# Sixteen modulation units as float32 weighted sums on VectorE, and a projection ring whose low part is written in place

## The reference, cut to what matters

```
mod   = silu(c)     @ w_ada + b_ada        # 1024 -> 6 * 1024
mod_c = silu(c_ctx) @ w_ada + b_ada
sh1, sc1, ga1, sh2, sc2, ga2 = split(mod, 6)
hl = rms_norm(x)   * (1 + sc1)  + sh1      # latents
hc = rms_norm(ctx) * (1 + csc1) + csh1     # context
```

## Time and profile before

| what | value |
|---|---|
| median of 3 runs | 1674.27 us (1671.4 to 1674.83) |
| span of the profiled execution | 1675.7 us |
| PE busy | 1390.9 us, 83% |
| DVE busy | 1021.4 us, 61% |
| ACT busy | 802.2 us, 48% |
| POOL busy | 133.2 us, 8% |
| mean granted TensorE clock | 0.916 |

### The profile page before, as it was taken

How to read it: one execution, slowest core, us unless ns; L and a number is a source line. 1 busy time by engine, 2 the same in 40 slices (tenths; PEclk the granted TensorE clock), 3 DMA queues, 4 the chain that set the end, 5 groups by cost and what they waited for, 6 DMA issues and landing times.

```text
span 1675.7 us, 23258 instructions
## 1 busy us (share of the span) xinstructions
PE 1390.9 (83%) x8782; PEld 1247.4 (74%) x8782; DVE 1021.4 (61%) x1204; ACT 802.2 (48%) x924; POOL 133.2 (8%) x126
## 2 busy tenths in 40 slices
PE   4797999796998989548588970699999999999980
PEld 2686899795898989437477950588889888898870
DVE  5638320598013332366732379688888888888865
ACT  5533220333122332536522231377887778887752
POOL 0000000210000000100000440100110001001103
PEclk9998989998998899879878995799999999999995
DMA  9110000002123323000040157599999999999965
GB/s 343 64 61 17 35 1 1 1 0 76 50 76 126 126 76 127 0 0 0 1 157 21 31 219 283 176 348 377 381 370 382 380 373 374 369 383 382 382 218 213
DMA packets 142118, 293.26 MB, mean 175 GB/s; under 512 B 4832, under 2 KB 94944, under 8 KB 139632
## 3 DMA queue, kind: packets, MB, share of 16 engines
q1 hardware_dynamic: 137456, 275.70, 45.5%
q0 software_dynamic: 4608, 16.78, 3.9%
HBM read 271.49 MB, written 20.97 MB: 175 GB/s over the span
## 4 chain that ended last, share of the span: by engine, by line
PE 68%; DVE 13%; ACT 5%; DMA 4%; issue 4%; SPq 3%; POOL 2%; DVEq 0%; POOLq 0%; ACTq 0%
PE psum L1870 18%; PE psum L1618 8%; PE psum L1659 5%; PE psum L1661 5%; PE psum L1660 5%; PE psum L1863 3%; PE psum L1861 3%; PE psum L1862 3%; SPq L517 2%; DMA e_raw<-w_e_up 2%; DVE w_lo L1054 2%; ACT w_hi L677 1%; DVE mask_add L1466 1%; DVE left L1469 1%; PE psum L1621 1%
## 5 line engine op out<-in xcount | busy, mean ns | idle before, releaser
L1486 DVE TENSOR_TENSOR e_lo<-e_raw,e_hi 128x2048 fp32r<-128x2048 f32 x192 | 434.1, 2288 | 50.9 <-ACT e_hi L987 49.8
L987 ACT ACTIVATE e_hi<-e_raw 128x2048 fp32r<-128x2048 f32 x192 | 363.5, 1914 | 76.6 <-PE psum L1870 46.3
L1659 PE MATMUL psum<-w_hi,h_hi 128*128 128x256 f32 x576 | 165.6, 287 | 0.5 <-issue 0.5
L1660 PE MATMUL psum<-w_hi,h_lo 128*128 128x256 f32 x576 | 164.5, 286 | 0.0
L1661 PE MATMUL psum<-w_lo,h_hi 128*128 128x256 f32 x576 | 164.4, 285 | 0.0
L1054 DVE TENSOR_TENSOR w_lo<-raw,w_hi 128x2048 fp32r<-128x2048 f32 x35 | 79.7, 2289 | 134.6 <-ACT w_hi L677 134.6
L1861 PE MATMUL psum<-e_hi,xt_hi 128*128 128x256 f32 x512 | 147.3, 288 | 0.0
L1863 PE MATMUL psum<-e_lo,xt_hi 128*128 128x256 f32 x512 | 144.8, 283 | 0.0
L1862 PE MATMUL psum<-e_hi,xt_lo 128*128 128x256 f32 x512 | 144.7, 283 | 0.0
L1659 PEld LDWEIGHTS psum<-w_hi,h_hi 128*128 128x128 f32 x576 | 112.3, 195 | 0.6 <-issue 0.6
L1660 PEld LDWEIGHTS psum<-w_hi,h_lo 128*128 128x128 f32 x576 | 112.1, 195 | 0.0
(11 more groups left out here) (343 smaller groups left out, 2965.2 us busy)
## 6 DMA issues: line engine op xcount, KB each, us to landing
e_raw<-w_e_gate SPq DMA_DIRECT2D x64, 1024.0 KB, 17.2
e_raw<-w_e_up SPq DMA_DIRECT2D x64, 1024.0 KB, 14.1
e_raw<-w_e_down SPq DMA_DIRECT2D x64, 1024.0 KB, 13.5
raw<-w_ada SPq DMA_DIRECT2D x16, 1024.0 KB, 5.5
raw<-w_in_units SPq DMA_DIRECT2D x15, 1024.0 KB, 4.8
ada_raw<-w_ada SPq DMA_DIRECT2D x8, 1024.0 KB, 12.2
xs<-x SPq DMA_DIRECT2D x4, 1024.0 KB, 13.8
raw<-w_out_units SPq DMA_DIRECT2D x4, 1024.0 KB, 5.0
```

The source lines that it names most:

```text
L987: act.activation(e_hi[u % EH][:], e_raw[u][:], ACT.Copy).then_inc(e_hi_ok, 1)
L1486: dve.tensor_tensor(e_lo[u][:], e_raw[u][:], e_hi[u % EH][:], ALU.subtract).then_inc(e_lo_ok, 1)
L1659: pe.matmul(o, x_hi[:, k, c], w_hi[n % 2][:, k, :], start=k == 0, stop=False)
L1660: pe.matmul(o, x_lo[:, k, c], w_hi[n % 2][:, k, :], start=False, stop=False)
```

## The change

Three edits go together.

1. The modulation units j = 8 to 23 leave the stream. They stand behind gq 2, gv0 3, gv1 3, o0 2, o1 2, r0 2 and r1 2. SP loads them to two raw buffers of their own (`ada_x`, at 16 and 24 KB of the ring). DVE multiplies each of the 8 blocks of 128 x 256 by its column of `c32` (silu of the latents' conditioning vector) and adds them up in float32 in `mod_acc` (four buffers): one `tensor_scalar` and seven `scalar_tensor_tensor`, each waiting for the one before. PE makes two products of 2 columns from the sum, with `one_c` (all ones), which adds over the partitions and lands as columns in `modps`. The context's column is no longer computed for these units. ACT has no part in it.
2. `w_lo[s]` has the address of `raw[s]`. The low part is written over the raw unit, and SP waits before loading unit n until PE has used unit n - 2 (`wait_used` moves from ACT to SP for n >= 10).
3. Addresses move: `h_ml`, `ml_ks`, `ml_c`, `sel_r` within the ring, and `pos_r2` to 16 KB of the ring. SP now loads `pos_r2` right behind `x_res`, and out2 and out3 behind `pos_r2`.

```diff
+ADA_COUNT = {"gq": 2, "gv0": 3, "gv1": 3, "o0": 2, "o1": 2, "r0": 2, "r1": 2}
...
+STREAM = [("ada", j) for j in ADA_FIRST] + [("in", j) for j in range(len(IN_UNITS))] + [("out", j) for j in range(4)]
...
-        w_hi = [at(f"w_hi{s}", AT_RING + (32 - 16 * s) * KB, [P, KC, UW], F32R) for s in range(2)]
-        w_lo = [at(f"w_lo{s}", AT_RING + (40 - 16 * s) * KB, [P, KC, UW], F32R) for s in range(2)]
+        w_lo = [at(f"w_lo{s}", AT_RING + 8 * KB * s, [P, KC, UW], F32R) for s in range(2)]
+        w_hi = [at(f"w_hi{s}", AT_RING + (32 + 8 * s) * KB, [P, KC, UW], F32R) for s in range(2)]
+        ada_x = [at(f"ada_x{s}", AT_RING + (16 + 8 * s) * KB, [P, KC, UW]) for s in range(2)]
+        mod_acc = at("mod_acc", AT_OUT + 58 * KB, [P, 4, UW])
...
             def load_unit(n):
                 if n >= 10:
-                    sp.wait_ge(hi_ready, n - 1)
-                    sp.wait_ge(lo_ready, n - 1)
+                    wait_used(sp, n - 2)
                 sp.dma_start(raw[n % 2][:], unit_src(*STREAM[n])).then_inc(raw_full[n % 2], 16)
...
             for n in range(EV_C0, AT["out", 0]):
                 load_unit(n)
-            for n in range(AT["out", 0], len(STREAM)):
+                for j in ADA_BEHIND.get(IN_UNITS[STREAM[n][1]], ()):
+                    if j == ADA_REST[0]:
+                        sp.wait_ge(ml_norm, 4)
+                    if j >= ADA_REST[2]:
+                        sp.wait_ge(ada_acc, j - 1)
+                    sp.dma_start(ada_x[j % 2][:], unit_src("ada", j)).then_inc(ada_x_full[j % 2], 16)
+            for n in range(AT["out", 0], AT["out", 2]):
                 load_unit(n)
...
             sp.wait_ge(yt_mm, KC)
             sp.dma_start(x_res[:], I["x"].rearrange("(t p) d -> p t d", p=P)).then_inc(s_xr, 16)
-            sp.wait_ge(hi_ready, len(STREAM))
-            sp.wait_ge(lo_ready, len(STREAM))
+            sp.wait_ge(ada_acc, 24)
             for half in range(2):
                 sp.dma_start(pos_r2[64 * half:64 * half + 64, :, :], ...).then_inc(s_pr, 16)
+
+            for n in range(AT["out", 2], len(STREAM)):
+                load_unit(n)
...
+            def ada_columns(name):                       # DVE
+                for j in ADA_BEHIND[name]:
+                    dve.wait_ge(ada_x_full[j % 2], 16 * ((j - ADA_REST[0]) // 2 + 2))
+                    if j >= ADA_REST[4]:
+                        dve.wait_ge(ada_cols, j - 3)
+                    o, w = mod_acc[:, j % 4, :], ada_x[j % 2]
+                    link(dve.tensor_scalar(o, w[:, 0, :], c32[:, 0, 0, 0:1], None, ALU.mult))
+                    for k in range(1, KC):
+                        i = dve.scalar_tensor_tensor(o, w[:, k, :], c32[:, 0, k, 0:1], o, ALU.mult, ALU.add)
+                        if k < KC - 1:
+                            link(i)
+                    i.then_inc(ada_acc, 1)
...
             split_lo(16)
+            ada_columns("gq")
             split_lo(17)
             for n in range(17, AT["out", 0]):
+                kind, j = STREAM[n]
+                name = IN_UNITS[j]
+                ada_columns(name)
                 if n + 1 < AT["out", 0]:
                     split_lo(n + 1)
...
+            def acc_to_cols(name):                       # PE
+                for j in ADA_BEHIND[name]:
+                    pe.wait_ge(ada_acc, j + 1)
+                    for r in range(2):
+                        i = pe.matmul(modps[:, 2 * j + r, :], mod_acc[:, j % 4, P * r:P * (r + 1)], one_c[:], start=True, stop=True)
+                    i.then_inc(ada_cols, 1)
+
             for n in range(17, AT["out", 0]):
...
+                name = IN_UNITS[STREAM[n][1]]
+                acc_to_cols(IN_UNITS[STREAM[n - 1][1]])
+                tok_unit(name, n, h_hi, h_lo, 0 if name[:2] == "gv" else TC)
+            acc_to_cols("r1")
```

More of the change, by code:

```diff
@@ L61 @@
 IN_UNITS = ["G", "k0", "k1", "q0", "q1", "v0", "v1", "gk", "gq", "gv0", "gv1", "o0", "o1", "r0", "r1"]
[L63 to L73, removed]
+ADA_COUNT = {"gq": 2, "gv0": 3, "gv1": 3, "o0": 2, "o1": 2, "r0": 2, "r1": 2}
+ADA_BEHIND = {}
+_j = ADA_REST[0]
+for _u, _k in ADA_COUNT.items():
+    ADA_BEHIND[_u] = list(range(_j, _j + _k))
+    _j += _k
+assert _j == 24
+STREAM = [("ada", j) for j in ADA_FIRST] + [("in", j) for j in range(len(IN_UNITS))] + [("out", j) for j in range(4)]
 AT = {("in", n): STREAM.index(("in", IN_UNITS.index(n))) for n in IN_UNITS}
-AT |= {("ada", j): STREAM.index(("ada", j)) for j in range(24)}
 AT |= {("out", j): STREAM.index(("out", j)) for j in range(4)}
@@ L144, in build @@
         one_s = small("one_s", [P, 2])
+        one_c = small("one_c", [P, 2])
         zero_r = small("zero_r", [P, P])
@@ L155, in build @@
         raw = [at(f"raw{s}", AT_RING + 8 * KB * s, [P, KC, UW]) for s in range(2)]
-        w_hi = [at(f"w_hi{s}", AT_RING + (32 - 16 * s) * KB, [P, KC, UW], F32R) for s in range(2)]
-        w_lo = [at(f"w_lo{s}", AT_RING + (40 - 16 * s) * KB, [P, KC, UW], F32R) for s in range(2)]
+        w_lo = [at(f"w_lo{s}", AT_RING + 8 * KB * s, [P, KC, UW], F32R) for s in range(2)]
+        w_hi = [at(f"w_hi{s}", AT_RING + (32 + 8 * s) * KB, [P, KC, UW], F32R) for s in range(2)]
+        a_hi = [at(f"a_hi{s}", AT_RING + (16 + 8 * s) * KB, [P, KC, UW], F32R) for s in range(2)]
+        ada_x = [at(f"ada_x{s}", AT_RING + (16 + 8 * s) * KB, [P, KC, UW]) for s in range(2)]
+        mod_acc = at("mod_acc", AT_OUT + 58 * KB, [P, 4, UW])
         xs = at("xs", AT_OUT, [P, TA, D])
@@ L179, in ml @@
         def ml(name, n):
-            return [at(f"{name}{d}", AT_RING + 2 * KB * (2 * n + d), [P, NH, P]) for d in range(2)]
+            return [at(f"{name}{d}", AT_RING + 2 * KB * (2 * n + d) + (16 * KB if n == 4 else 0), [P, NH, P]) for d in range(2)]
         ml_w, ml_sw, ml_qs, ml_kh, ml_ks = ml("ml_w", 0), ml("ml_sw", 1), ml("ml_qs", 2), ml("ml_kh", 3), ml("ml_ks", 4)
-        ml_c = at("ml_c", AT_RING + 20 * KB, [P, 2, NH, HD + 1])
-        h_ml = at("h_ml", AT_RING + 32 * KB, [P, TL, ML_W])
-        sel_r = at("sel_r", AT_RING + 28 * KB, [P, 2 * NH, P], F32R)
+        ml_c = at("ml_c", AT_RING + 36 * KB, [P, 2, NH, HD + 1])
+        h_ml = at("h_ml", AT_RING + 16 * KB, [P, TL, ML_W])
+        sel_r = at("sel_r", AT_RING + 44 * KB, [P, 2 * NH, P], F32R)
         h_sq = at("h_sq", AT_OUT + 34 * KB, [P, TL, ML_W])
@@ L235, in build @@
         mod1_ready = sem("mod1_ready")
+        ada_x_full, ada_acc = [ada_full[6], ada_full[7]], ada_evac
         ssq_done, std_done, xn_ready = sem("ssq_done"), sem("std_done"), sem("xn_ready")
@@ L246, in split_bufs @@
             if n < 8:
-                return (w_hi + w_lo)[n % 4], ada_lo[n]
+                return (w_hi + a_hi)[n % 4], ada_lo[n]
             return w_hi[n % 2], w_lo[n % 2]
@@ L367, in build @@
         x_res = at("x_res", AT_OUT, [P, TL, D])
-        pos_r2 = at("pos_r2", AT_RING, [P, TL, D // 2])
+        pos_r2 = at("pos_r2", AT_RING + 16 * KB, [P, TL, D // 2])
         pos_c2 = at("pos_c2", AT_OUT + 64 * KB, [P, D // 2])
@@ L559, in _ @@
             pool.memset(one_s[:], 0.0).then_inc(konst, 1)
+            pool.memset(one_c[:], 1.0)
             pool.wait_ge(konst, 4)
@@ L674, in split_hi @@
                     src = raw[n % 2]
-                if n >= (2 if n >= 8 else 4):
-                    wait_used(act, n - (2 if n >= 8 else 4))
+                if n in (8, 9):
+                    wait_used(act, n - 2)
+                elif 4 <= n < 8:
+                    wait_used(act, n - 4)
                 act.activation(split_bufs(n)[0][:], src[:], ACT.Copy).then_inc(hi_ready, 1)
@@ L813, in _ @@
             act.activation(c32[:, 0, :, :], cc, ACT.Silu).then_inc(c_again, 1)
[L815 to L820, removed]
             act.wait_ge(ml_norm, 4)
@@ L1245, in _ @@
             dve.wait_ge(c_again, 1)
-            link(dve.memset(c_st[:].bitcast(F32), 0.0))
-            link(dve.tensor_copy(c_st[:, :, 0:2], c32[:, 0, :, :]))
-            dve.tensor_tensor(c_st[:, :, 2:4], c32[:, 0, :, :], c_st[:, :, 0:2], ALU.subtract).then_inc(c_ready, 1)
             dve.wait_ge(ml_norm, 4)
+            def ada_columns(name):
[10 more added lines that the diff above has]
+                    i.then_inc(ada_acc, 1)
             split_lo(16)
+            ada_columns("gq")
             split_lo(17)
             for n in range(17, AT["out", 0]):
+                kind, j = STREAM[n]
+                name = IN_UNITS[j]
+                ada_columns(name)
                 if n + 1 < AT["out", 0]:
                     split_lo(n + 1)
-                kind, j = STREAM[n]
-                if kind == "ada" or IN_UNITS[j][0] == "r":
+                if name[0] == "r":
                     continue
-                name = IN_UNITS[j]
                 p0, pairs = PAIRS[name]
@@ L1718, in _ @@
             pe.wait_ge(g_free, 6)
-            pe.wait_ge(c_ready, 2)
-            for n in range(17, AT["out", 0]):
[L1721 to L1736, removed]
+            def acc_to_cols(name):
```

(6 more changed lines are left out.)

5 lines of the change are left out of this document (removed).

## The result

The changed kernel takes 1621.24 us (median of 4 runs, 1618.51 to 1622.58) against 1674.49 us (1671.4 to 1674.83) for the kernel before: ratio 0.9685, 95% interval 0.9663 to 0.9707. That is 53.3 us less; the forecast was 1618 us, which is 56.3 less by its sum. The profiled execution took 1622.58 us, with a span of 1620.8.

What follows compares the result with a forecast made beforehand. PE bounds the kernel, held by the ring in modulation blocks. Span 1675.7 - 64.3 + 4.0 (unit 10) + 4 (POOL clash) = 1619.4 us; the profile stood 1.4 over the median, so 1618 us, range 1609 to 1630.

Steps and rivals of the forecast that it cites:

- The stretch from gq to r1: From gq's end to r1's end, PE's work alone would take 157.0 us against 221.3: 64.3 us gone.
- The small products: Sixteen pairs of products from the sums on PE, 0.34 us each at full clock, 5.4 us in the stretch.
- Sums hidden: DVE's eight steps, 3.8 us a unit, lie beside PE's token units; even 1.2 us a step would close in time.
- this rival: DVE's sums slower than their slot: delay from about 1.2 us a step, whole gain eaten at 1.5; 1734 us, chance 0.03.
- The in-place ring: Units ready 9.7 us after the load's start, against 23 us units: no cost, except early unit 10, 4.0 us lost.
- ACT's splits and copies, SP's sixteen more DMAs: ACT losing 16 splits and 16 copies gives nothing while PE binds; sixteen more DMAs on SP cost nothing.
- No gain from POOL's earlier additions: At out3, PE's pair and POOL's addition came together, a tie, so adding position rows earlier gains nothing.
- The clash with POOL: In the output projection, POOL's earlier additions delay `make_diag(1)`, for which PE waits: 4 us lost, range 0 to 9.
- The rule of the Trainium skill: By it POOL's addition stops the diagonal, giving the 4 us term; with only shared bandwidth, under 1 us.

Runs made afterwards that it cites:

- the repeated one: The changed kernel measured once more without any edit, as base for the kernels beside it: 1617.4 us, ratio 0.9673 to the kernel before.
- unit 10 early: Changed kernel with unit 10 loaded early to a third raw buffer at 16 KB of the ring: 1614.25 us, ratio 0.9647.
- the additions were laid over it: Changed kernel with POOL's first addition held until the last pair of out0 is done: 1626.11 us, ratio 0.9716.
- the sums two and three times: Changed kernel with DVE computing every weighted sum twice (1618.75 us, ratio 0.9669) or three times (1635.4 us, ratio 0.9766).
- The kernel with half products: Kernel before, with the sixteen later modulation units multiplied by their high part only: 1676.9 us, ratio 1.0016.
- the two that keep the modulation units on PE: Kernel before with only the changed one's ring, addresses and SP order (1716.86 us), and kernel before with high-part products only (1676.9 us).

## Why the prediction was right

Its steps, one by one:

- *The stretch from gq to r1*: forecast 64.3 us less, measured 62.4. The mechanism was right in every part: PE alone on the chain, sums and loads beside it. Two terms were undersized. The small products took 5.9 us in the stretch (and 0.8 more just behind its end), not 5.4, since the 0.34 us of the earlier trace rows was the part of four records that lay on the chain between others, while a run of eight costs 0.79 and the first one 1.05. And gv0 took 30.4 us and not 28.9: its first pair came 7.4 us after the small products, where 5.8 is usual, in a window with a granted clock of 0.82; I had counted the clock as full from the start.
- *Sums hidden*: 3.96 us a unit against 3.8, hidden at twice the length. The place from which they decide was put at 1.2 us a step; at 0.97 nothing showed, at 1.46 it was 17.9 us. Wrong was the second number of this rival, that 1.5 us a step would eat the whole gain: it put all sixteen units in the stretch, while j = 8 to 11 are mostly done before it begins.
- *The in-place ring*: hidden for every unit but number 10. Its price was 4.0 us and measured 3.3: I took 5.4 us from use to split, a value with another wait in it, and it was 4.7 (117.16 to 121.90).
- *ACT's splits and copies, SP's sixteen more DMAs*: nothing, as said. ACT's 35 us less busy time bought no time.
- *No gain from POOL's earlier additions*: right, the first pair of out3 is still bound by PE. Only the forecast of "some 45 us earlier relative to out0" was a slip: from the copy of row product 0 to POOL's first addition it was 70.7 us and became 17.2, which is 53 earlier, as the prediction's own 929.6 and 877 give.
- *The clash with POOL*: right in place and mechanism; its size of 4 us was the weakest number, and it was too large. The diagonal lost 0.46 us in the first profile, 1.2 in the repeated one, 2.1 with unit 10 early, and 7.3 when the additions were laid over it. PE's two waits for diagonals, 5.6 us together before, were 6.0 and 6.8 in the two traces of the changed kernel, and 6.3 and 7.4 with the sums two and three times: 0.4 to 1.8 us more. The landing was forecast well: the additions began 23.6 us after the loads were issued at 796.66, the forecast had 24 (852.8 to 877). But 9 us of instruction against a need at 883.5 in the earlier trace rows leaves 2.5 by the prediction's own numbers, and the need itself came 31.9 us after that issue and not 30.7, closer to the addition's end.
- *The clock behind the gap* had no term of its own here, and no run shows it to be the change's. In the first profile the row product behind the wait of 3.2 us took 3.78 us and not the 2.62 of the earlier trace rows, and the stage 2.7 us more than before. In the repeated one the wait was longer, 4.0 us, but the row product took 2.86 and the stage 1.0 us less than before. The kernel with half products has the late part of the kernel before unchanged and took 103.62 us there, at a granted clock of 0.98, where the kernel before took 106.44 at 0.95.
- *The rule of the Trainium skill* (page "SBUF — State Buffer", section "Who interferes with whom"), that two SBUF inputs on VectorE and a reading GpSimd instruction exclude each other for the whole instruction: the runs agree in each overlap. The diagonal took 1.68, 3.30 and 8.53 us instead of 1.22 in the lines above, and a low part 7.34 and 11.02 instead of 2.29; and they agree with its other half, that one SBUF input doesn't contend (0.68 to 0.69 us for the multiplication of a pair, under an addition or not).

By what was measured at the steps, the sum would have been -62.4 + 3.3 + 0.4 to 1.8, that is 57.3 to 58.7 us less and not 56.3: the stretch was forecast 1.9 us too good, unit 10 and the clash together 2.9 to 4.3 us too bad, and the errors partly cancel. The medians differ by 53.3 us in the first measurement. The rest of the difference lies in parts for which no edit is shown to be the cause. Three of them vary under the same code: the first part up to G's end, the GLA (135.2 to 136.9 us), and the output projection. The experts took 1.5 us less after the change, and 0.4 to 1.7 less in each of the other eight traces, the two that keep the modulation units on PE among them (612.95 and 611.72 us); why is open. So the mechanism and the great term were forecast; that the total came within 3.2 us of one median and 0.6 of the other (1621.24 and 1617.4) is in part luck.

## What to carry to other kernels

Before moving work off an engine that a trace shows as busy, ask what ends each of its waits: here half of the products could go and the blocks became only 4.9 us shorter, because a ring of load, split and low part set their pace, and taking the short units out of the ring gave 62 us with the same bytes and more work on DVE. A buffer that is reused in place is loaded later by the whole time of its user; list the units by length, and look at the first one, where the next engine used to find its data waiting. Where a profile has TensorE idle for 3 us between two long runs, look at the granted clock behind the gap too: two gaps of 6.0 to 7.7 us together, each closed by moving one operation of 1.2 us forward, were worth 9.5 to 13.8 us in the traces, since PE's own work also fell, from between 98.7 and 103.1 us to 95.9.

## What the runs showed of the hardware that I had not expected

- Shortening PE's work inside wait-bound blocks went with a lower granted clock of the stretch (0.92 to 0.86). The blocks became 4.9 us shorter, the unchanged token units behind them 8.5 us longer, and the stretch 3.6 us longer.
- VectorE and GpSimd took turns: after DVE's diagonal had waited for an addition of 8.81 us, POOL's next addition waited for the diagonal (9.90 instead of 9.04 us), and DVE's low part then waited for that addition (11.02 instead of 2.29 us).
- A gap of the same kind does not always lower the clock: behind a wait of 3.25 us the row product took 3.78 us, behind one of 3.97 us in another execution of the same kernel 2.86, and without a gap 1.88.
- The same code took 135.2 us in the GLA stage in some executions and 136.8 in others, and the whole kernel 1611.6 to 1621.5 us. A difference of 3 us is seen in one wait of a trace, not in six timed runs.
